# The 64x64 inverse of a chunked RWKV-7 scan, built on diagonal 32x32 blocks in place of whole chunks

## What is computed

```python
def step(s, inp):
    r_t, w_t, k_t, v_t, a_t, b_t = inp
    sa = jnp.einsum('bhij,bhj->bhi', s, a_t)
    s = s * w_t[:, :, None, :] + sa[..., None] * b_t[:, :, None, :] + v_t[..., None] * k_t[:, :, None, :]
    return s, jnp.einsum('bhij,bhj->bhi', s, r_t)
```

## Time and profile before

| | us |
|---|---|
| median of 3 runs | 3266.66 (3264.73 to 3270.63) |
| profiled execution, own time | 3264.91 |
| its span | 3263.3 |
| PE busy | 3107.3 (95%) |
| DVE / ACT / POOL busy | 1656.5 / 939.4 / 294.1 |
| the scan, first to last matmul | 1177.07 to about 1404 |

### The profile page before, as it was taken

The page is one execution under the profiler, slowest core; times in us unless marked ns, Lnnn a source line. Parts: engine busy times, 40 slices in busy tenths (PEclk is TensorE's granted clock), DMA queues, the critical chain, the costliest instruction groups (busy, mean ns, idle before and its releaser), DMA issues. The chain is left out here.

```text
span 3263.3 us, 61887 instructions
## 1 busy us (share of the span) xinstructions
PE 3107.3 (95%) x25826; PEld 2937.6 (90%) x25826; DVE 1656.5 (51%) x2929; ACT 939.4 (29%) x1742; POOL 294.1 (9%) x326
## 2 busy tenths in 40 slices
PE   7999999998999989978898989999998999999998
PEld 6999999998999989837676669999998999999998
DVE  4454444546544746656654453343435554445545
ACT  5212122114211422244655352221244111111113
POOL 0000000004100212230002100000023000000003
PEclk8999999999999999988999999999999999999999
DMA  6111111103422220002013641112134111111103
GB/s 190 47 39 51 51 40 50 39 26 101 144 83 79 67 86 5 18 3 64 7 53 120 232 179 52 49 49 53 37 96 130 39 39 58 44 51 39 39 26 104
DMA packets 257468, 218.60 MB, mean 67 GB/s; under 512 B 41688, under 2 KB 235009, under 8 KB 256634
## 3 DMA queue, kind: packets, MB, share of 16 engines
q1 hardware_dynamic: 252410, 196.33, 19.6%
q0 software_dynamic: 3824, 19.47, 1.7%
q10 hardware_dynamic: 1040, 0.00, 0.0%
HBM read 179.81 MB, written 35.96 MB: 66 GB/s over the span
## 5 line engine op out<-in xcount | busy, mean ns | idle before, releaser
L1484 PE MATMUL banks<-XR,wR 128*128 128x344 f32 x6336 | 1004.8, 320 | 5.9 <-DVE rs L1598 4.3
L1484 PEld LDWEIGHTS banks<-XR,wR 128*128 128x128 f32 x6336 | 998.9, 188 | 6.5 <-issue 3.1
L1484 PE MATMUL banks<-hidR,wR 128*128 128x344 f32 x3168 | 511.1, 321 | 2.9 <-DVE tiles L1718 2.9
L1484 PEld LDWEIGHTS banks<-hidR,wR 128*128 128x128 f32 x3168 | 500.6, 188 | 9.2 <-DVE tiles L1718 4.7
L1567 ACT ACTIVATE sq<-sq 128x344 f32<-128x344 f32 x120 | 59.2, 493 | 927.1 <-DVE sq L1596 927.1
L1618 DVE TENSOR_TENSOR tiles<-tiles,banks 128x344 f32<-128x344 f32 x480 | 240.4, 511 | 166.1 <-PE banks L1484 165.2
L1095 PE MATMUL banks<-XR,pR 128*128 128x344 f32 (+1 forms) x1944 | 318.4, 325 | 3.6 <-DVE pR L2208 2.9
L1095 PEld LDWEIGHTS banks<-XR,pR 128*128 128x128 f32 (+1 forms) x1944 | 311.7, 191 | 10.2 <-issue 6.1
L1095 PE MATMUL banks<-XR,mg_gate 128*128 128x344 f32 x1728 | 283.3, 319 | 1.3 <-PEq L53 1.3
L1095 PEld LDWEIGHTS banks<-XR,mg_gate 128*128 128x128 f32 x1728 | 273.8, 188 | 1.6 <-issue 1.6
L1596 DVE TENSOR_TENSOR sq<-banks,shared 128x344 f32<-128x344 f32 x120 | 61.9, 516 | 365.7 <-PE banks L1484 365.6
(11 more groups left out here) (481 smaller groups left out, 3936.4 us busy)
## 6 DMA issues: line engine op xcount, KB each, us to landing
wraw<-in_ffn_down SPq DMA_DIRECT2D x22, 1024.0 KB, 4.8
wraw<-in_ffn_gate SPq DMA_DIRECT2D x43, 512.0 KB, 3.7
wraw<-in_ffn_up SPq DMA_DIRECT2D x43, 512.0 KB, 4.8
praw<-in_w_in SPq DMA_DIRECT2D x26, 512.0 KB, 4.2
tiles<-h_spill SPq DMA_DIRECT2D x9, 1376.0 KB, 6.9
sq<-in_w_in SPq DMA_DIRECT2D x24, 512.0 KB, 4.0
tiles<-in_cache_mla SPq DMA_DIRECT2D x64, 144.0 KB, 3.1
tiles<-in_cache_mla POOLq DMA_DIRECT2D x64, 144.0 KB, 3.2
```

The lines of the kernel that those rows point to most:

```text
L1484: ins = self.k.nc.tensor.matmul(out, wgt[:, a, cols], x(b)[:, grp(g)], start=first and n == 0, stop=last and n == 2)
```

## The change

Levels 2 to 16 work on the two 32x32 diagonal blocks of each head's matrix alone. Tiles `Tm`, `Tt`, `Gm`, `NT_` and `Ym` are 128 partitions by 4 x 32: both heads and both blocks side by side, j = 0 to 3 on the partitions. A product is now 4 x 4 matmuls of 32x32, each on the diagonal 32x32 tile of the array that belongs to its partitions. N is needed only in these blocks for those levels, transposed and not, and `gram_blocks` computes both afresh from 64-row by 32-column pieces (64 matmuls of 64x32 with 32 moving columns for the pair, where `g3` had 16 of 64x64). After level 16 VectorE puts the four blocks in their places in the 64x64 `TT` (zeroed once by GpSimd), and level 32 is one corner per head: Y = G1 corner times T of the first block, then times the second, 8 + 8 matmuls of 32x32 per chunk; ScalarE copies the corner into `TT` (a new step, `corner`, for which `solved` and the gram product `g2` of the next pair now wait). GpSimd has 4 masks of 128x128 per chunk in place of 5 of 128x256. The pieces of the old pair stand in one place per level, between `inner` and `outer`; before, some stood behind `outer`, and VectorE's `state(b)` moves from ahead of level 16's adds to the end of the period.

```diff
-        pe_steps += [("g1", p), ("g3", p), ("g2", p)] if this else []
+        pe_steps += [("g1", p), ("blocks", p), ("g2", p)] if this else []
...
+    def piece(t, j, h, lo=0):
+        return t[BLK * j:BLK * (j + 1), h, lo:lo + BLK]
...
+            def gram_blocks(p):
...
+                for n in R2:
+                    for h in H4:
+                        for i in R2:
+                            for s in R2:
+                                for q in R2:
+                                    c = 2 * p + s
+                                    j = 2 * side(c, q) + i
+                                    left, right = (now(k.A, 4, c), now(k.A, 0, c)) if n == 0 else (now(k.A, 0, c), now(k.A, 4, c))
+                                    ins = mm(piece(blocks(Gb[s], n * NB), j, h), lane(left, h, q, BLK * i, BLK),
+                                             lane(right, h, q, BLK * i, BLK))
+                pe_s.done(ins, ("blocks", p))
...
             def inner(p, s, l):
...
-                pe_s.done(both(lambda h, q: mm(lane(half(Yb[s], 0, CH), h, q), lane(NT_[s], h, q), lane(Tm[s], h, q))),
-                          ("Y", p, s, l))
+                for h in H4:
+                    for j in range(4) if l < LV[-1] else (1, 3):
+                        left = piece(NT_[s], j, h) if l < LV[-1] else piece(G1[p % 2][s], j - 1, h, BLK)
+                        ins = mm(piece(blocks(Yb[s], 0), j, h), left, piece(Tm[s], j if l < LV[-1] else j - 1, h))
...
             def outer(p, s, l):
...
-                if l < LV[-1]:
-                    both(lambda h, q: mm(lane(half(Zb[s], 0, CH), h, q), lane(TT[z][s], h, q), lane(Ym[s], h, q)))
-                pe_s.done(both(lambda h, q: mm(lane(half(Zb[s], NU, CH), h, q), lane(Ym[s], h, q), lane(TT[z][s], h, q))),
-                          ("Z", p, s, l))
+                for m in R2 if l < LV[-1] else (1,):
+                    for h in H4:
+                        for j in range(4) if l < LV[-1] else (1, 3):
+                            if l == LV[-1]:
+                                ins = mm(piece(blocks(Zb[s], NB), j - 1, h), piece(Ym[s], j, h), piece(TT[z][s], j, h, BLK))
+                            elif m:
+                                ins = mm(piece(blocks(Zb[s], NB), j, h), piece(Ym[s], j, h), piece(Tt[s], j, h))
+                            else:
+                                mm(piece(blocks(Zb[s], 0), j, h), piece(Tt[s], j, h), piece(Ym[s], j, h))
...
@@ scalar @@
+                for s in R2 if this else ():
+                    pe_s.wait(act, ("Z", p, s, LV[-1]))
+                    for q in R2:
+                        at = slice(64 * q, 64 * q + BLK)
+                        ins = nc.scalar.activation(TT[z][s][at, :, BLK:CH], blocks(Zb[s], NB)[at], ACT.Copy)
+                    act_s.done(ins, ("corner", p, s))
@@ vector @@
+                        if l < LV[-2]:
+                            ins = nc.vector.tensor_tensor(Tt[s], Tt[s], blocks(Zb[s], NB), ALU.add)
+                        else:
+                            for j in range(4):
+                                at = slice(BLK * j, BLK * (j + 1))
+                                lo = BLK * (j % 2)
+                                ins = nc.vector.tensor_tensor(TT[z][s][at, :, lo:lo + BLK], Tt[s][at], blocks(Zb[s], NB)[at], ALU.add)
```

More of the change, by code:

```diff
@@ L243 @@
 CH = 64
+BLK = CH // 2
 NCH = SEQ // CH
@@ L298, in four, with two @@
         return [[view(area, at + (2 * z + s) * RT * c, c) for s in R2] for z in R2]
-    def two(at):
-        return [view(work, at + s * NU, CH) for s in R2]
+    def two(at, c=CH):
+        return [view(work, at + s * RT * c, c) for s in R2]
     G1, G2 = four(room, 0, 2 * CH), four(room, 8 * NU, 2 * CH)
@@ L335, in rwkv_scan @@
-        pool_steps += [("level", p, s, 2) for s in R2] if this else []
-        pool_steps += [("level", p, s, l) for l in LV[1:] for s in R2] if this else []
+        dve_steps += [(m, p, s) for m in ("G1", "Tm", "Tt", "TmI", "first", "G2") for s in R2] if this else []
+        pool_steps += [("level", p, s, l) for l in LV[:-1] for s in R2] if this else []
         for l in LV:
             pe_steps += [("Y", p, s, l) for s in R2] if this else []
-            pe_steps += {2: [("S", a)], 4: [("W", b)], 8: [("U", b)], 16: [("S", b)]}.get(l, []) if past else []
+            pe_steps += {2: [("S", a)], 4: [("from_state", b)], 8: [("W", b), ("O", a)], 16: [("U", b), ("read", b)],
+                         32: [("S", b), ("O", b)]}[l] if past else []
@@ L346, in rwkv_scan @@
+            dve_steps += [("sum", a), ("state", a)] if past and l == 2 else []
+            dve_steps += [("T", p, s, l) for s in R2] if this and l < LV[-1] else []
+            dve_steps += [("sum", b), ("state", b)] if past and l == LV[-1] else []
+        act_steps += [("corner", p, s) for s in R2] if this else []
     pe_s, act_s, dve_s = Steps(k, "scan_products", pe_steps), Steps(k, "scan_copies", act_steps), \
@@ L506, in inner @@
                 i = LV.index(l)
-                pool_s.wait(pe, ("level", p, s, l))
                 dve_s.wait(pe, ("T", p, s, LV[i - 1]) if i else ("TmI", p, s))
@@ L528, in _ @@
                     gram(p, "g1")
-                    gram(p, "g3")
+                    gram_blocks(p)
                     gram(p, "g2")
@@ L574, in _ @@
                         if l == 32:
-                            output(b, (2, 3))
+                            state(b)
+                            output(b, H4)
+                    elif l == 4:
+                        sample.turn(pe, (3, 4, 5))
+                    if this:
+                        outer(p, 0, l)
+                        outer(p, 1, l)
         @block.scalar
@@ L589, in one @@
                     copy(out, x, step, step)
+                if this:
+                    for s in R2:
+                        copy(Gm[s], blocks(Gb[s], 0), ("Gm", p, s), ("blocks", p))
                 if past:
```

126 lines of the change are left out of this document (58 added, 68 removed).

## The result

| | before | after |
|---|---|---|
| median (lowest to highest), us | 3265.72 (3264.73 to 3270.63), 4 runs | 3387.32 (3380.62 to 3388.68), 4 runs |
| ratio | | 1.0365, 95% interval 1.0347 to 1.0383: slower |
| profiled execution, span | 3264.91, 3263.3 | 3386.04, 3384.0 |
| instruction packets of queue q8, whole kernel | 147 | 176 |

The change costs 121.6 us. The page of the changed kernel, where the earlier trace rows shows 25826 records of PE: 3840 more, which is the forecast 1920 matmuls (5504 in place of 3584), two records of each kind for one.

A forecast was written before the change was run, and what follows sets the result against it. It took the arrival of PE's code in 256-instruction blocks as the bound: +91.6 us for periods 1 to 7 and +5.5 for period 0, the rest 0, make +97 on 3264.91, called 3364; range 3320 to 3400.

The forecast's parts named there:

- Step (1): PE's program in the scan: 688 matmuls a period in place of 448, 10.83 blocks of 256 instructions; 5504 matmuls for 3584.
- Step (2): Small 32x32 matmuls on PE: 7.6 to 15 ns each, a block 1.0 to 2.0 us of array time, so blocks' arrival decides.
- rival B: Small matmuls on PE can't start closer than about 25 ns: +52 and +3 us for period 0, 3322; chance 0.08.
- rival C: Small tiles on PE don't overlap: 27.9 us in place of 13.6, +14.3 a period, 3380; chance 0.05.
- Step (3): Time per block of PE code in the scan: 3.7 us, bounds 3.46 and 4.10; periods 1 to 7 +91.6 us.
- Rival A: Code arrives in time and PE's array decides: faster, 3236, if a block takes under 2.49 us; chance 0.08.
- sign of being wrong: In the scan: instruction packets closer than 3.3 us, or 128 small records without a stall behind them.
- Step (4): Level 16's adds on 32 partitions and corner copies: cost 0, hidden in waits for code; without that cover up to 15 us.
- Step (5): Old pair's pieces moved one place later, between a level's products, VectorE reaching `state(b)` later: cost 0.
- Period 0: First period of the scan: 560 matmuls for 320, 8.87 blocks, 32.8 us for 27.3, +5.5; sample-step waits may add.
- Rival D: Clock falls as PE starves in the scan: at most +9 us a period, half likely, 3395 and up; chance 0.10.
- The other signs: In the scan: PE issue waits 8 to 12 us a period; VectorE, ScalarE, GpSimd fewer busy us, longer waits on PE.

The follow-up runs named there:

- short 32x32: Kernel before, plus 240 matmuls per period of 32x32 weights on four diagonal tiles with one moving column, in periods 1 to 7; 3371.45 us, ratio 1.0325.
- old order: Changed kernel with the order of before: some of the old pair's pieces behind `outer`, VectorE's state step of chunk b at level 16; 3379.17 us, ratio 1.0343.
- level 32 later: Changed kernel with the old pair's last pieces (state and output of chunk b, `read_state`) moved ahead of level 32's `inner`; 3378.46 us, ratio 1.0346.

## Why the prediction was right, and where it was short

The forecast was 3364, slower, for the time in which code arrives; 3387.3 is within the range and 23 us above the forecast.

**Step (1), the length of the program**, held: 10.83 blocks a period, 87 packets forecast for the scan and 86 found, 29 more in the whole kernel for 1920 x 4/256 = 30.

**Step (2), the pace of small matmuls**, held: 10.7 ns, between the bounds of 7.6 and 15, and of no weight in the sum. That removes rival B (no floor of 25 ns, nor of 15) and rival C (small tiles do overlap).

**Step (3), the time of a block**, held as a mechanism. Two experiments that leave the rest alone price it from both sides: 4.1 us for each of 26 packets more, 3.55 for each of 18 fewer (3.8 and 3.3 by the profiled scans), where the array's own time would give about two fifths to a half of that. Rival A would have needed less than 2.49. The prediction's sign of being wrong was packets closer than 3.3 us; the closest two of the changed kernel are 3.32 apart. Read from the starts of the instruction packets, with the granted clock of the stretch in which each block is used (number of intervals in brackets):

| | periods 1 to 7, us | shortest, mean interval | mean at clock 1.00 | mean below 0.75 |
|---|---|---|---|---|
| before | 188.85 | 3.35, 3.82 | 3.82 (48) | none |
| changed | 296.9 | 3.32, 3.91 | 3.74 (23) | 4.03 (37) |
| short 32x32 | 289.0 | 3.28, 3.81 | 3.77 (47) | 3.98 (14) |
| old order | 287.8 | 3.34, 3.79 | 3.77 (20) | 3.79 (36) |
| level 32 later | 290.8 | 3.30, 3.82 | 3.71 (23) | 3.85 (37) |

The rule of the Trainium skill (Runtime: NRT & Kernel Launch, Instruction fetch mechanics) that crossing a block's boundary is mostly hidden doesn't hold for small matmuls: 72.3 us of a scan of 345 are issue waits. The size was a little low: 296.9/75.8 = 3.92 us a block for the 3.70 taken, 16.4 us over seven periods. Of these 6 to 9 belong to the next two steps; the rest, 7 to 10 us, is the block's: 3.7 had been taken from the quicker windows, and the mean of 3.78 in the earlier trace rows was the better number.

**Step (4), cost 0 for the adds on 32 partitions: this step failed, by 6 to 9 us.** Its bounds held: 1.40 us a chunk for at most 2.1, a wait of 1.38 us a period for at most 2.2. What failed is the argument that a wait inside a block delays nothing, because it counted on slack that isn't there at the lower clock. The block with level 32's waits goes on with `state(b)` and `output(b)`, 64 records on two tiles. In period 4, where these run at 1.00 and 30 ns, the two intervals there are 3.9 and 4.2 us. In periods 1, 2, 3 and 6, at a clock of 0.50 to 0.53 and some 53 ns a record, 64 records alone are 3.4 us, the waits come on top, and the interval is 5.2 to 5.9 us, as here in period 2:

```profile
1301.80:1307.20 5.40, 4.91 (x108) 4.74 (x110) 3.00 (x9) 0.76 (x4) 0.00 (x0) 0.50 0.02 3
```

Moving that work ahead of the waits gave back 8.9 us of the median, 6.1 in periods 1 to 7.

**Step (5), cost 0 for the order: failed likewise,** 8.1 us in the changed kernel, 19.7 in the kernel before. I had looked at who waits for `state(b)`, and not at what the pieces had covered in their old places, the turn-around behind each level's `outer`. What (5) and (4) cost may be in part the same us.

**Period 0** was costed at 5.5 us and took 10.6. No experiment went into it; its waits on the sample step were named as what might add to it, and this stays a guess. Its granted clock is 0.64 for 0.92 before, which may have a part.

**Rival D** foresaw the clock: 0.69 to 0.79 in periods 1 to 7. It isn't what made most of the time. With the old order the clock is as low (0.74 over periods 1 to 7), and its intervals are 3.79 us below 0.75 and 3.77 at 1.00; in the changed kernel the difference of 0.29 us over 37 intervals is 11 us, most of it in the blocks at level 32. That the clock alone made this difference isn't shown: it comes together with the waits of steps (4) and (5).

**The other signs.** PE waited by issue for 9 us a period, as forecast. The wrong one is ScalarE, which was to have fewer busy us: it has 56.5 in periods 1 to 7 for 53.6, since the copies are shorter but four corner copies per pair have come in.

In sum, of the 23.6 us of span that the 97 missed: 16.4 in periods 1 to 7 (6 to 9 the waits and the order, the rest the block), 5.1 in period 0, 5.2 ahead of the scan and -3.2 from the drain on; of these last two all but 0.3 lie outside the code of the change. The errors of the sum nearly all add up; it was not luck that kept it in the range, but a range that was wide enough.

## What to carry to other kernels

Before splitting matmuls into smaller ones, count the instructions: an f32 matmul is four of them, and no two instruction packets in the scans read above are less than 3.28 us apart, so that under some 26 ns a matmul record (3.28/128) the array's saving is lost. A wait is free only if the block in which it lies has slack, at the clock that is granted there, so put the waits beside the small matmuls and cover them with nothing that fills a block by itself. And where removed waits come back as "issue", look at the packets of the instruction queue before weaving further.

## What the runs showed of the hardware

- PE's program arrives in packets of 256 instructions, and in five kernels no two are less than 3.28 us apart; the mean is 3.8 to 3.9 us, at a granted clock of 1.00 as at 0.50 to 0.75 (3.77 and 3.79 us with the old order).
- At a granted clock of 1.00, small f32 matmuls of 32x32 weights on four diagonal tiles start 10.7 ns apart with 32 columns and 8.6 ns with one; of 64x64 weights on two tiles 28.7 ns with one column, 29.2 with 64. The tile's size and number set the pace here, hardly the columns.
- On two 64x64 tiles the pace was 30 ns at a granted clock of 1.00 and 53 ns at 0.50.
- Going from 64x64 to 32x32 tiles the next record started 148 ns after the last, back again 95 ns after.
- Alternating 128x128 and 128x64 tiles cost 122 ns a record (granted clock 0.83), 15 for the same transposes in equal 64x64 tiles.
- A semaphore increment as an instruction of its own on PE took 155 ns.
- An add of VectorE on 32 partitions by 128 elements took 0.28 us, as long as one on 128 partitions by 128 (0.29).
- The granted clock was 0.69 to 0.79 in the periods of the changed kernel, and 0.85 to 0.96 with ten wide matmuls added per period, without a gain in time.
